# Second norm of an encoder layer: most token rows normed and stored before the last expert pair ends, that pair's tokens normed in slot order and scattered

## The chip, the cores and the metric

The kernel runs on one core of one Trainium2 chip. The metric is the device time of one launch in microseconds (us), the median of repeated runs of one program. Engines are named as the profile names them: PE is TensorE (PEld its weight loads), DVE is VectorE, ACT is ScalarE, POOL is GpSimd, and SP is SyncE, which here issues nearly all transfers.

## The reference

One encoder layer on T = 384 tokens (256 prompt tokens and 8 streams of 16), D = 1024, all in f32: a token mixer, a norm (LN1) that gives h, a mixture of 32 experts of which each token takes four, and a second norm (LN2):

```python
h = layer_norm(DEEPNORM_ALPHA * x + m, ln1_g, ln1_b)
f = moe(h.reshape(B * L, D), w_router, b_router, w_gu, b_gu, w_down, b_down).reshape(B, L, D)
y = layer_norm(DEEPNORM_ALPHA * h + f, ln2_g, ln2_b)
...
gu = xb @ w_gu[e] + b_gu[e]              # (1024 -> 2 x 1024)
h = (up + 1.0) * gate * jax.nn.sigmoid(SWIGLU_ALPHA * gate)   # after clamping
return h @ w_down[e] + b_down[e]
```

A token's LN2 needs its mean and variance over all 1024 channels, and so the outputs of all four of its experts. Each expert has 12 MB of weights, of which all must be read: 16 pairs of experts read 16 x 24 MB.

## The kernel before

The tokens stand as NT = 3 tiles of 128 partitions. After the mixer, the kernel goes over 16 pairs of experts (`pair`). An expert has SLOTS = 64 slots for its tokens, so a pair fills the 128 partitions: slots 0 to 63 belong to expert a = 0, slots 64 to 127 to a = 1. `onehot` (tokens by slots) says which token sits in which slot. It is built for the next pair on DVE (`slots_of`), and `gather` on PE multiplies `hid` (which holds h) by it to give `xg`.

In a pair, PE does this in order:

- `gate_up(0)`, in eight chunks c of 128 input channels, and between its chunks 4 and 6 the scatter of the pair before (`combine`: slot outputs `oo_hi` and `oo_lo` times the transposed one-hot `gt`, added into `xy` by DVE in `add_outputs`), and `gates`, which makes `gt` for this pair.
- `gate_up(1)`, with the transposes of expert 0's activations at chunk 4.
- `down(0)`, with expert 1's transposes at chunk 4.
- `gather` for the next pair (not in the last pair).
- `down(1)`.

The matrices' f32 products have 64 stationary columns, one half of the output columns in partitions 0 to 63 of a bank and the other half (`hf`) in partitions 64 to 127. The trace shows each f32 matmul as two instructions.

SP issues the weights in pieces into a ring of 16 rooms of 1 MB (`ring`, `old_rooms`), each into a room as soon as PE has used what lay there (`piece_used`), so up to 16 MB are ordered ahead. All these transfers and the stores of `y` are issued from SP. The last pair's last piece of `w_down` is split in two (`last_low_full` for chunks 4 and 5 of `down(1)`, L541).

`xy` (tokens by channels) starts as ALPHA * h and has every pair's outputs added. In the last pair, before the change, `xy` is split into a high and a low part (ACT at L1298, DVE `low_sums` at L1806), and PE adds these into six banks through an identity (`sums_so_far`, L1056 and L1061). After `down(1)` PE adds the last pair's outputs on top (L1123, L1127), so the banks hold all sums in token order. Then LN2 of all three tiles follows: `half_stats` and `row_stats` on DVE, `row_rstd` on POOL, `centre` (L1883) and `finish` (L1898) on DVE for tiles 1 and 2, ACT (L1349) and POOL (L1407, L1409) for tile 0, tile 2's variance on ACT (`squares`). The six stores of 256 KB are at L614. LN2's gain and offset (`lnp`, 1 MB as broadcast) are loaded by ACT at L1313 late in the last pair.

In this code `last_down` and all names with `late_` are new, and the functions named above for the norm after the loop are gone.

## Time and profile before

| What | us |
| --- | --- |
| Median of 3 runs | 1114.89 (1114.82 to 1115.33) |
| Profiled execution, own device time | 1111.98 |
| Profiled execution, span (first to last instruction) | 1109.9 |
| PE busy in the span | 1070.8 |
| Mean granted TensorE clock | 0.996 |
| DMA mean rate over the span | 393 GB/s |
| Last instruction of the last `down(1)` ends | 1094.05 |
| First store of `y` issued | 1102.51 |

All positions in the trace are us from the start of the span. A timeline row gives the start, the time that the run of instructions is busy, the engine, the line, the operation and its tiles and shapes, how many, and in brackets the engine's idle time before it and what ended it. Consecutive matmuls overlap, so the duration of one is longer than its share.

### The profile page before, as it was taken

How to read it: one execution, taken by the hardware profiler on the slowest of the kernel's cores; microseconds unless marked ns; L12 is line 12 of the kernel's file. 1: busy time of each engine (PE TensorE's matmuls, PEld its weight loads, DVE VectorE, ACT ScalarE, POOL GpSimd, SP SyncE). 2: the span in 40 equal slices, each digit the busy share in tenths (PEclk: the TensorE clock that was granted, in tenths of full speed). 3: DMA queues.
4: the chain of work that ended last, by engine and by line, in shares of the span. 5: the costliest groups of instructions: out<-in, count | busy, mean ns of one | idle time of the engine just before them, and what ended most of it. 6: DMA issues, size and time to landing. Idle time of an engine off the chain costs nothing.

```text
span 1109.9 us, 13640 instructions
## 1 busy us (share of the span) xinstructions
PE 1070.8 (96%) x5552; PEld 543.4 (49%) x5552; DVE 327.8 (30%) x601; ACT 207.4 (19%) x361; POOL 90.2 (8%) x50
## 2 busy tenths in 40 slices
PE   9999999999999999999999999999898989898995
PEld 6889988353434343444443434343434343342532
DVE  3487765512121212121213121212131312112134
ACT  3243334120202020202020101020111111110122
POOL 4675500000000000000000000000000000000002
PEclk9999999999999999999999999999999999999998
DMA  9972778999999999999999999999999999999994
GB/s 351 324 244 76 247 306 347 393 424 411 427 429 424 430 427 427 427 426 429 428 428 428 427 429 427 427 429 429 427 429 427 427 429 429 425 428 430 425 428 193
DMA packets 56611, 436.27 MB, mean 393 GB/s; under 512 B 8128, under 2 KB 18112, under 8 KB 29088
## 3 DMA queue, kind: packets, MB, share of 16 engines
q1 hardware_dynamic: 50048, 428.68, 93.2%
q10 hardware_dynamic: 6528, 7.09, 1.9%
q8 instruction: 26, 0.43, 0.2%
q14 instruction: 9, 0.07, 0.0%
HBM read 431.78 MB, written 3.97 MB: 393 GB/s over the span
## 4 chain that ended last, share of the span: by engine, by line
PE 67%; DMA 25%; DVE 1%; issue 0%; POOL 0%; ACT 0%; POOLq 0%; SPq 0%; DVEq 0%
PE bank L1014 25%; DMA ring<-w_down 25%; PE bank L1046 18%; PE bank L946 8%; PE bank L639 5%; PE bank L1075 1%; PE bank L995 1%; PE bank L866 1%; PE bank L1077 1%; PE bank L1023 1%; PE bank L856 1%; PE bank L802 1%; PE bank L782 1%; PE bank L788 1%; PE bank L805 1%; PE bank L806 1%
## 5 line engine op out<-in xcount | busy, mean ns | idle before, releaser
L1014 PE MATMUL bank<-ring,xg 128*64 128x512 f32 x1536 | 345.3, 595 | 7.3 <-DMA ring<-w_gu 7.1
L1014 PEld LDWEIGHTS bank<-ring,xg 128*64 128x64 f32 x1536 | 105.0, 136 | 209.1 <-issue 187.9
L1046 PE MATMUL bank<-ring,act_t 128*64 128x512 f32 x672 | 151.0, 595 | 8.3 <-DMA ring<-w_down 8.3
L1014 PE MATMUL bank<-old_rooms,xg 128*64 128x512 f32 x496 | 112.4, 595 | 4.9 <-DMA old_rooms<-w_gu 4.9
L1786 DVE SCALAR_TENSOR_TENSOR oo_lo<-oo_raw,gate_s,oo_hi 128x512 fp32r<-128x512 f32 x32 | 24.0, 751 | 309.7 <-ACT oo_hi L1290 309.7
L1822 DVE TENSOR_SCALAR gate_c<-bank 128x512 f32<-128x512 f32 x32 | 22.1, 691 | 251.3 <-PE bank L1014 251.3
L946 PEld LDWEIGHTS bank<-onehot,hid 128*128 128x128 f32 x720 | 85.9, 196 | 12.2 <-issue 12.2
L1046 PEld LDWEIGHTS bank<-ring,act_t 128*64 128x64 f32 x672 | 46.1, 137 | 92.8 <-issue 78.0
L946 PE MATMUL bank<-onehot,hid 128*128 128x128 f32 x720 | 88.8, 283 | 0.0
L1800 DVE TENSOR_TENSOR xy<-xy,bank 128x512 f32<-128x512 f32 x84 | 52.7, 682 | 107.6 <-PE bank L1077 107.6
L1382 POOL TENSOR_TENSOR rstd<-veps,minus_half 128x1 f32<-128x1 f32 x6 | 3.3, 544 | 960.3 <-DVE veps L1582 960.0
L1365 POOL TENSOR_TENSOR w_parts<-ring,w_parts 128x1024 fp32r<-128x1024 f32 x27 | 74.5, 2762 | 52.9 <-ACT w_parts L1161 52.9
L1014 PEld LDWEIGHTS bank<-old_rooms,xg 128*64 128x64 f32 x496 | 34.1, 136 | 68.2 <-issue 57.4
L1317 ACT COPY oo_raw<-bank 64x512 f32<-64x512 f32 x63 | 36.5, 580 | 159.9 <-PE bank L1046 159.1
L1046 PE MATMUL bank<-old_rooms,act_t 128*64 128x512 f32 x256 | 58.4, 595 | 4.1 <-DMA old_rooms<-w_down 4.1
L1301 ACT ACTIVATE sig<-gate_c 128x512 f32<-128x512 f32 x32 | 20.2, 630 | 179.1 <-DVE gate_c L1822 179.1
L1303 ACT COPY act_t<-bank 128x512 f32<-128x512 f32 x32 | 18.7, 585 | 165.7 <-PE bank L995 165.7
L1279 ACT CAST gt<-bank 128x384 fp32r<-128x384 f32 x16 | 7.7, 479 | 201.2 <-PE bank L958 201.2
L639 PE MATMUL bank<-w_parts,x_hi 128*128 128x512 f32 x180 | 45.1, 397 | 0.0
L1161 ACT CAST w_parts<-ring 128x1024 fp32r<-128x1024 f32 x27 | 28.4, 1053 | 65.8 <-PE bank L639 60.3
L1075 PE MATMUL bank<-oo_hi,gt 128*128 128x512 f32 x90 | 38.5, 428 | 0.0
L639 PEld LDWEIGHTS bank<-w_parts,x_hi 128*128 128x128 f32 x180 | 33.7, 187 | 8.8 <-issue 0.8
(258 smaller groups left out, 940.1 us busy)
## 6 DMA issues: line engine op xcount, KB each, us to landing
ring<-w_gu SPq DMA_DIRECT2D x90, 2048.0 KB, 30.5
ring<-w_down SPq DMA_DIRECT2D x41, 2048.0 KB, 33.0
old_rooms<-w_gu SPq DMA_DIRECT2D x30, 2048.0 KB, 30.3
old_rooms<-w_down SPq DMA_DIRECT2D x18, 1024.0 KB, 26.4
old_rooms<-w_down SPq DMA_DIRECT2D x7, 2048.0 KB, 32.1
ring<-w_in SPq DMA_DIRECT2D x13, 1024.0 KB, 14.5
ring<-w_gu SPq DMA_DIRECT2D x12, 1024.0 KB, 6.2
over_q<-w_down SPq DMA_DIRECT2D x3, 2048.0 KB, 15.9
```

The source lines that it names most:

```text
L639: mm = pe.matmul(out, lhs, rhs, start=(n == 0 and c == 0), stop=(n == 2 and c == KC - 1))
L946: mm = pe.matmul(bank[6 + c // 4][:, (c % 4) * 128:(c % 4 + 1) * 128], hid[:, t, :].rearrange("p (q m k) -> p q k m", m=128, k=GU_RUN) [:, ...
L1014: mm = pe.matmul(bank[2 * a + n][64 * hf:64 * hf + 64, :], xg[:, c, 64 * a:64 * a + 64], w[:, col:col + 512], start=False, stop=(c == KC - 1))
L1046: mm = pe.matmul(bank[b][64 * hf:64 * hf + 64, :], act_t[:, a, c % 4, 64 * (c // 4):64 * (c // 4) + 64], w[:, c % run, hf * 512:(hf + 1) * ...
L1075: pe.matmul(bank[comb_banks[i]][:, :], gt[:, t * 128:(t + 1) * 128], oo_hi[:, hf, :], start=True, stop=False)
L1161: act.copy(w_parts[:, n % PARTS, 0, :], w).then_inc(w_hi_ready, 1)
L1301: act.activation(sig[:, :], gate_c[:, :], ACT.Sigmoid, scale=SIG).then_inc(sig_ready, 1)
L1317: act.copy(oo_raw[64 * a:64 * a + 64, hf, :], bank[down_banks[a]][64 * hf:64 * hf + 64, :]).then_inc(out_ready, 1)
L1365: pool.tensor_tensor(w_parts[:, n % PARTS, 1, :], w, w_parts[:, n % PARTS, 0, :].bitcast(F32), ALU.subtract).then_inc(w_lo_ready, 1)
L1786: dve.scalar_tensor_tensor(oo_lo[:, hf, :], oo_raw[:, hf, :], gate_s[:, 0:1], oo_hi[:, hf, :].bitcast(F32), ALU.mult, ALU.subtract).then_i ...
L1800: dve.tensor_tensor(xy[:, t, o], xy[:, t, o], bank[comb_banks[i]][:, :], ALU.add)\
L1822: dve.tensor_scalar(gate_c[:, :], bank[2 * a][:, :], LIMIT, None, ALU.min).then_inc(gate_ready, 1)
```

## The change

The last pair is no longer scattered by PE into token order. Instead:

- **Norm tables.** ACT loads only one row each of gain and offset (8 KB) at the start of the pair before the last. PE spreads them over 128 partitions by products with a row of ones (`last_norm_rows`, at chunks 2 and 6 of that pair's `gate_up(1)`), and ACT copies them to `lnp`.
- **Rows without the last pair.** In the last pair DVE takes the statistics of `xy` (`row_norm`), norms all three tiles (`norm_early`) and SP stores them whole (three stores of 512 KB), also the rows of tokens that the last pair still changes.
- **Slots.** `gates` is left out in the last pair. PE makes small tables instead (`late_slots`): each slot's token number and gates, and which slots of the two experts hold the same token. `late_rows` gathers each slot's sum so far from `xy`. `last_down` does the product of expert 1 in column halves q of 256 (in bank 5 and bank 7), so that the half q = 0 is complete before q = 1.
- **Norm in slot order.** A slot's row of 1024 lies as two halves of 512 in partitions s and 64 + s. Expert 0's slots are normed first (`late_norm(0)`), and what expert 0 adds to a token that is in expert 1 too goes over by `late_cross`. Half rows' statistics are brought together by small products with the identity (`late_stats`). Expert 1's slots follow.
- **Scatter.** POOL writes the two sets of 128 half rows (256 KB each) to `y` with two indirect transfers, once the three plain stores have landed. Slots that must not be written have an index out of bounds.

The split of `xy` into high and low parts, `sums_so_far`, the products at L1123 and L1127, and everything after the loop are gone.

```diff
+        pe_gain, pe_offset, pe_slots, pe_rows, pe_cross, pe_half, pe_moments = (1, 2), (3, 4), 5, (6, 7), 8, 10, (9, 11)
+        act_gain, act_offset, act_values, act_rows, act_split, act_scaled = 1, 2, 3, (4, 5), 6, 7
+        dve_table, dve_index, dve_stats, dve_rows = 1, 2, (3, 5), (4, 6)
+        last_banks = (5, 7)
...
-            for t, n in ((1, 0), (1, 1), (0, 0), (2, 0), (2, 1), (0, 1)):
-                if t == 0:
-                    sp.wait_ge(y_pool, n + 1)
-                else:
-                    sp.wait_ge(y_done, 2 * (t - 1) + n + 1)
-                o = slice(n * 512, (n + 1) * 512)
-                sp.dma_start(y_out[t * 128:(t + 1) * 128, o], xy[:, t, o]).then_inc(rows_stored, 16)
-            sp.wait_ge(rows_stored, 16 * (2 * NT + 1))
+            for t in range(NT):
+                sp.wait_ge(y_done, 2 * t + 2)
+                sp.dma_start(y_out[t * 128:(t + 1) * 128, :], xy[:, t, :]).then_inc(rows_stored, 16)
+            sp.wait_ge(rows_stored, 16 * (NT + 1))
+            sp.wait_ge(late_stored, 32)
...
+            def last_down(turn):
+                for q in range(2):
+                    for hf in range(2):
+                        pe.matmul(bank[last_banks[q]][64 * hf:64 * hf + 64, 0:256], sel_down[:, 1, :],
+                                  biasp[:, 2 * FF + hf * 512 + q * 256:2 * FF + hf * 512 + q * 256 + 256],
+                                  start=True, stop=False)
+                for c in range(KC):
+                    if c == 4:
+                        late_cross()
...
+                        order = [(k, q) for q in range(2) for k in (c, c + 1)]
+                    elif c < KC - 2:
+                        order = [(c, q) for q in range(2)]
+                    else:
+                        order = []
+                    for k, q in order:
+                        for hf in range(2):
+                            col = hf * 512 + q * 256
+                            mm = pe.matmul(bank[last_banks[q]][64 * hf:64 * hf + 64, 0:256],
+                                           act_t[:, 1, k % 4, 64 * (k // 4):64 * (k // 4) + 64],
+                                           w[:, k % DN_RUN, col:col + 256], start=False, stop=(k == KC - 1))
+                        if (k, q) == (KC - 1, 0):
+                            mm.then_inc(late_pe, 1)
+                    if c % 2 == 1:
+                        mm.then_inc(piece_used, 1)
...
+            def late_slots():
+                pe.wait_ge(late_dve, dve_table)
+                for e in range(2):
+                    for hf in range(2):
+                        for t in range(NT):
+                            pe.matmul(bank[6 + e][64 * hf:64 * hf + 64, 0:4], onehot[:, t, 64 * e:64 * e + 64],
+                                      late_tab[:, t, :], start=(t == 0), stop=(t == NT - 1))
-                    pe.matmul(bank[last_banks[2 * t + hf]][:, :], ident_r, sums_hi[:, t, hf * 512:(hf + 1) * 512],
-                              start=True, stop=False)
-                pe.wait_ge(sums_lo_ready, t + 1)
+                    for t in range(NT):
+                        mm = pe.matmul(bank[5][64 * hf:64 * hf + 64, 0:SLOTS], onehot[:, t, 0:64],
+                                       onehot[:, t, 64:128], start=(t == 0), stop=(t == NT - 1))
+                mm.then_inc(late_pe, 1)
+            row_ones = cst[0:1, C_IOTA + 1:C_IOTA + 2].to_broadcast([1, 128])
+            def late_rows(e):
+                if e == 0:
+                    pe.wait_ge(late_act, act_values)
+                for t in range(NT):
+                    for hf in range(2):
+                        mm = pe.matmul(bank[6 + e][64 * hf:64 * hf + 64, :], onehot[:, t, 64 * e:64 * e + 64],
+                                       xy[:, t, hf * 512:(hf + 1) * 512], start=(t == 0), stop=(t == NT - 1))
+                mm.then_inc(late_pe, 1)
+            def last_norm_rows(n, p):
+                if n == 0:
+                    pe.wait_ge(ln2_in, 16)
+                    pe.wait_ge(gate_ready, 2 * p + 1)
+                    pe.wait_ge(up_ready, 2 * p + 1)
+                else:
+                    pe.wait_ge(late_act, act_gain)
-                    o = slice((2 * t + hf) * 512, (2 * t + hf + 1) * 512)
-                    pe.matmul(bank[last_banks[2 * t + hf]][:, :], ident_r,
-                              x_lo[:, :, :].rearrange("p k t -> p (k t)")[:, o], start=False, stop=False)
+                    pe.matmul(bank[hf][:, :], row_ones, lnp[0:1, n, hf * 512:(hf + 1) * 512], start=True, stop=True)\
+                        .then_inc(late_pe, 1)
+            def late_stats(e):
+                pe.wait_ge(late_dve, dve_stats[e])
+                w = 6 * (1 + e)
+                for half in range(2):
+                    for hf in range(2):
+                        mm = pe.matmul(bank[1 + e][64 * hf:64 * hf + 64, w * half:w * half + w],
+                                       ident[:, 64 * half:64 * half + 64], late_stat[:, e, 0:w], start=True, stop=True)
+                mm.then_inc(late_pe, 1)
+            def late_cross():
+                pe.wait_ge(late_act, act_scaled)
+                for hf in range(2):
+                    r = slice(64 * hf, 64 * hf + 64)
+                    mm = pe.matmul(bank[0][r, :], late_same[r, :], late_out[r, :], start=True, stop=True)
+                mm.then_inc(late_pe, 1)
+                late_stats(0)
...
+                        {4: lambda: upper_and_combine(p), 6: lambda: combine_and_slots(p)} if last else
...
-                        | ({2: lambda: sums_so_far(0), 6: lambda: sums_so_far(1)} if last else {})
+                        | ({1: lambda: late_rows(0), 2: lambda: late_rows(1)} if last else {})
+                        | ({2: lambda: last_norm_rows(0, p), 6: lambda: last_norm_rows(1, p)} if tables else {})
...
+                    late_stats(1)
...
+            def norm_tables(n):
+                for hf in range(2):
+                    act.wait_ge(late_pe, (pe_gain, pe_offset)[n][hf])
+                    ins = act.copy(lnp[:, n, hf * 512:(hf + 1) * 512], bank[hf][:, :])
+                ins.then_inc(late_act, 1)
+            def pair(p, first=False, tables=False):
+                if tables:
+                    act.dma_start(lnp[0:1, :, :], ln2.rearrange("(a n) d -> a n d", a=1)).then_inc(ln2_in, 16)
...
+            def last_pair_of(p):
+                act.wait_ge(late_pe, pe_slots)
+                for e in range(2):
+                    act.copy(late_val[:, e, :], bank[6 + e][:, 0:4])
+                act.copy(late_same, bank[5][:, 0:SLOTS]).then_inc(late_act, 1)
+                activations(p, 0)
+                act.wait_ge(xg_ready, 2 * p)
+                for e in range(2):
+                    act.wait_ge(late_pe, pe_rows[e])
+                    act.copy(late_x[e], bank[6 + e][:, :]).then_inc(late_act, 1)
+                copy_act_t(p, 0)
+                act.wait_ge(late_act, act_offset)
+                for hf in range(2):
+                    r = slice(64 * hf, 64 * hf + 64)
+                    ins = act.copy(late_gb[r, :, :], lnp[r, :, hf * 512:(hf + 1) * 512])
+                ins.then_inc(late_act, 1)
+                activations(p, 1)
+                copy_act_t(p, 1)
+                act.wait_ge(late_act, act_values)
+                act.wait_ge(piece_used, PAIR_PIECES * p + MIX_PIECES + 2 * GU_PIECES + DN_PIECES)
+                act.activation(late_out, bank[down_banks[0]][:, :], ACT.Copy, scale=late_val[:, 0, 2:3])\
+                    .then_inc(late_act, 1)
...
+            for e in range(2):
+                pool.wait_ge(ln_var, 2 * NT + e + 1)
+                pool.tensor_tensor(late_rstd[:, e:e + 1], late_ve[:, e:e + 1], minus_half[:, 0:1], ALU.pow)\
+                    .then_inc(ln_rstd, 1)
+            rows = y_out.rearrange("t (h n) -> (t h) n", h=2)
+            pool.wait_ge(late_dve, dve_index)
+            pool.wait_ge(rows_stored, 16 * (NT + 1))
+            for e, done in enumerate((late_sum, up_c[:, :])):
+                pool.wait_ge(late_dve, dve_rows[e])
+                pool.indirect_dma_start(rows, bass.IndirectOffsetOnAxis(ap=late_idx[:, e:e + 1], axis=0), done, None,
+                                        bounds_check=2 * T - 1, oob_is_err=False).then_inc(late_stored, 16)
...
+            def row_norm(t):
+                for n in range(2):
+                    ins = dve.bn_stats(stat[:, t, n, :], xy[:, t, n * 512:(n + 1) * 512])
+                link(ins)
+                row_stats(t, NT + t + 1)
+            def norm_early(t):
+                dve.wait_ge(late_act, act_gain)
+                for n in range(2):
+                    o = slice(n * 512, (n + 1) * 512)
+                    dve.scalar_tensor_tensor(xy[:, t, o], xy[:, t, o], mv[:, t, 0:1], lnp[:, 0, o],
+                                             ALU.subtract, ALU.mult).then_inc(y_centred, 1)
+                dve.wait_ge(ln_rstd, NT + t + 1)
+                dve.wait_ge(late_act, act_offset)
+                for n in range(2):
+                    o = slice(n * 512, (n + 1) * 512)
+                    dve.wait_ge(y_centred, 2 * t + n + 1)
+                    dve.scalar_tensor_tensor(xy[:, t, o], xy[:, t, o], rstd[:, t:t + 1], lnp[:, 1, o],
+                                             ALU.mult, ALU.add).then_inc(y_done, 1)
+            def row_index():
+                dve.wait_ge(late_act, act_values)
+                for e in range(2):
+                    ins = dve.tensor_tensor(late_idx[:, e:e + 1], late_val[:, e, e:e + 1], late_half, ALU.add)
+                ins.then_inc(late_dve, 1)
+            def late_norm(e, done):
+                s = bank[(6, 3)[e]][:, :]
+                dve.wait_ge(late_pe, pe_moments[e])
+                link(dve.bn_aggr(late_mv[:, e, :], bank[1 + e][:, 0:12 * (1 + e)]))
+                dve.tensor_scalar_add(late_ve[:, e:e + 1], late_mv[:, e, 1:2], EPS).then_inc(ln_var, 1)
+                link(dve.scalar_tensor_tensor(s, s, late_mv[:, e, 0:1], late_gb[:, 0, :], ALU.subtract, ALU.mult))
+                dve.wait_ge(ln_rstd, 2 * NT + e + 1)
+                dve.scalar_tensor_tensor(done, s, late_rstd[:, e:e + 1], late_gb[:, 1, :], ALU.mult, ALU.add)\
+                    .then_inc(late_dve, 1)
+            def late_outputs(p):
+                dve.wait_ge(late_act, act_scaled)
+                link(dve.tensor_tensor(bank[6][:, :], late_out, late_x[0], ALU.add))
+                dve.bn_stats(late_stat[:, 0, 0:6], bank[6][:, :]).then_inc(late_dve, 1)
+                dve.wait_ge(late_pe, pe_cross)
+                link(dve.tensor_tensor(late_x[1], late_x[1], bank[0][:, :], ALU.add))
+                late_norm(0, late_sum)
+                for q in range(2):
+                    o = slice(256 * q, 256 * q + 256)
+                    if q == 0:
+                        dve.wait_ge(late_pe, pe_half)
+                    else:
+                        dve.wait_ge(piece_used, PAIR_PIECES * p + MIX_PIECES + PAIR_PIECES)
+                    link(dve.scalar_tensor_tensor(bank[3][:, o], bank[last_banks[q]][:, 0:256], late_val[:, 1, 3:4],
+                                                  late_x[1][:, o], ALU.mult, ALU.add))
+                    ins = dve.bn_stats(late_stat[:, 1, 6 * q:6 * q + 6], bank[3][:, o])
+                ins.then_inc(late_dve, 1)
+                late_norm(1, up_c[:, :])
```

How this moves instructions: first PE in the last pair, from the end of `combine` to the start of `down(0)`. Before (`gates` is L955 and L958, `sums_so_far` L1056 and L1061):

```order
L955 MATMUL bank<-gate,onehot 128x2 x3
L958 MATMUL bank<-cst,onehot 128x128 x3
L1014 MATMUL bank<-old_rooms,xg 64x512 x8
L1099 REGISTER_ALU
L866 MATMUL bank<-biasp,sel 64x512 x4
L1014 MATMUL bank<-old_rooms,xg 64x512 x8
L1056 MATMUL bank<-over_r 128x512 x2
L1061 MATMUL bank<-x_lo,over_r 128x512 x2
L1014 MATMUL bank<-ring,xg 64x512 x8
L995 MATMUL bank<-cst,act_h 128x128 x4
L1014 MATMUL bank<-ring,xg 64x512 x8
```

And after (L1107 and L1111 are `late_slots`, L1123 `late_rows`):

```order
L1107 MATMUL bank<-rank_all,onehot 64x4 x12
L1111 MATMUL bank<-onehot 64x64 x6
L1026 MATMUL bank<-old_rooms,xg 64x512 x8
L1200 REGISTER_ALU
L878 MATMUL bank<-biasp,sel 64x512 x4
L1026 MATMUL bank<-old_rooms,xg 64x512 x4
L1123 MATMUL bank<-xy,onehot 64x512 x6
L1026 MATMUL bank<-old_rooms,xg 64x512 x4
L1123 MATMUL bank<-xy,onehot 64x512 x6
L1026 MATMUL bank<-ring,xg 64x512 x8
```

Six matmuls of `gates` became 18 small ones, and eight of `sums_so_far` (two turns of four) became twelve f32 ones with 64 stationary columns.

The end of PE's program, from expert 1's down product on. Before:

```order
L1023 MATMUL bank<-biasp,sel_down 64x512 x2
L1046 MATMUL bank<-ring,act_t 64x512 x8
L1038 ISA
L1046 MATMUL bank<-old_rooms,act_t 64x512 x8
L1123 MATMUL bank<-oo_hi,gt 128x512 x3
L1127 MATMUL bank<-oo_lo,gt 128x512 x3
L1123 MATMUL bank<-oo_hi,gt 128x512 x3
L1127 MATMUL bank<-oo_lo,gt 128x512 x3
```

And after (L1093 is `last_down`, L1154 `late_cross`, L1145 `late_stats`):

```order
L1068 MATMUL bank<-biasp,sel_down 64x256 x4
L1093 MATMUL bank<-ring,act_t 64x256 x16
L1154 MATMUL bank<-hid,rank_all 64x512 x2
L1145 MATMUL bank<-rank_all,cst 64x6 x4
L1078 ISA
L1093 MATMUL bank<-old_rooms,act_t 64x256 x16
L1145 MATMUL bank<-rank_all,cst 64x12 x4
```

The twelve products that scattered the last pair are gone from behind the down product. Two products of `late_cross` and four small ones stand in its middle, and only four small ones behind it.

POOL's last rows. Before:

```order
L1382 TENSOR_TENSOR rstd<-veps,minus_half 128x1 x5
L1407 TENSOR_TENSOR xy<-xy,lnp 128x512
L1409 TENSOR_TENSOR xy<-xy,lnp 128x512
L1382 TENSOR_TENSOR rstd<-veps,minus_half 128x1
L1407 TENSOR_TENSOR xy<-xy,lnp 128x512
L1409 TENSOR_TENSOR xy<-xy,lnp 128x512
```

And after (`late_rstd` lies in `rank_all`, L1517 are the two scatters):

```order
L1502 TENSOR_TENSOR gg<-wr,ln_t 128x8x32 x2
L1487 TENSOR_TENSOR rstd<-veps,minus_half 128x1 x6
L1510 TENSOR_TENSOR rank_all<-rank_all,minus_half 128x1 x2
L1517 DMA y<-hid,late_idx 768x512
L1517 DMA y<-up_c,late_idx 768x512
```

POOL's four passes over tile 0 are gone, and both scatters stand behind both powers, the second scatter behind the first.

## Rows read from the trace of the kernel before

**Rows 1.** The page, part 1: busy time, share, instructions.
```profile
PE 1070.8 (96%) x5552; PEld 543.4 (49%) x5552; DVE 327.8 (30%) x601; ACT 207.4 (19%) x361; POOL 90.2 (8%) x50
```

**Rows 2.** Timeline of PE, pair ahead of the last: start, us, engine, line.
```profile
1000.07 7.31 PE L1014 MATMUL bank<-ring,xg 128*64 128x512 f32 x32
...
1008.61 3.65 PE L1014 MATMUL bank<-ring,xg 128*64 128x512 f32 x16 [0.56 <-DMA ring<-w_gu]
1013.51 3.65 PE L1014 MATMUL bank<-old_rooms,xg 128*64 128x512 f32 x16 [1.25 <-DMA old_rooms<-w_gu]
...
1018.42 3.65 PE L1046 MATMUL bank<-old_rooms,act_t 128*64 128x512 f32 x16 [1.03 <-DMA old_rooms<-w_down]
...
1023.32 3.65 PE L1046 MATMUL bank<-ring,act_t 128*64 128x512 f32 x16 [0.57 <-DMA ring<-w_down]
```

**Rows 3.** Windows of the stream's end: busy us, clock, DMA share, GB/s.
```profile
1084.00:1086.00 2.00, 2.00 (x10) 0.99 (x12) 0.00 (x0) 0.00 (x0) 0.00 (x0) 1.00 1.01 422
...
1091.00:1092.00 1.00, 1.00 (x8) 0.31 (x6) 0.00 (x0) 0.00 (x0) 0.00 (x0) 1.00 0.02 8
```

**Rows 4.** Timeline of PE, last pair.
```profile
1053.94 0.72 PE L955 MATMUL bank<-gate,onehot 128*128 128x2 f32 x6
...
1054.98 3.65 PE L1014 MATMUL bank<-old_rooms,xg 128*64 128x512 f32 x16
...
1062.43 0.73 PE L1056 MATMUL bank<-over_r 128*128 128x512 f32 x2
...
1063.56 3.65 PE L1014 MATMUL bank<-ring,xg 128*64 128x512 f32 x16
...
1077.17 3.65 PE L1046 MATMUL bank<-ring,act_t 128*64 128x512 f32 x16 [0.77 <-DMA ring<-w_down]
...
1082.05 1.94 PE L1046 MATMUL bank<-ring,act_t 128*64 128x512 f32 x8 [0.55 <-DMA ring<-w_down]
```

**Rows 5.** The chain that ended last, last pair.
```profile
1047.52 34.49 DMA ring<-w_down
...
1087.19 6.89 PE bank L1046 x32
```

**Rows 6.** Lines by form, PE: count, busy us, mean ns.
```profile
L946 PE MATMUL bank<-onehot,hid 128*128 128x128 f32 x720 | 88.8, 283 | 0.0
...
L725 PE MATMUL bank<-st,hid 128*32 128x128 f32 x64 | 2.6, 279 | 0.0
```

**Rows 7.** Lines by form, DVE.
```profile
L1603 DVE BATCH_NORM_STATS2 stat<-hid 128x6 f32<-128x512 f32 x6 | 4.2, 695 | 0.2
...
L1516 DVE BATCH_NORM_STATS2 gst<-bank 128x6 f32<-128x128 f32 x12 | 2.7, 283 | 2.7 <-PE bank L725 2.7
...
L1571 DVE SCALAR_TENSOR_TENSOR qkt<-bank,chn,zu 128x256 f32<-128x256 f32 x4 | 1.9, 476 | 7.0 <-PE bank L639 7.0
```

**Rows 8.** Timeline of the tail, all engines.
```profile
1098.99 0.21 DVE L1581 BATCH_NORM_AGGREGATE mv<-stat 128x2 f32<-128x12 f32 x1
...
1099.23 0.15 DVE L1582 TENSOR_SCALAR veps<-mv 128x1 f32<-128x1 f32 x1
...
1099.47 0.54 POOL L1382 TENSOR_TENSOR rstd<-veps,minus_half 128x1 f32<-128x1 f32 x1 [916.66 <-DVE veps L1582]
...
1100.43 1.41 DVE L1883 SCALAR_TENSOR_TENSOR bank<-bank,mv,lnp 128x512 f32<-128x512 f32 x2
...
1101.35 1.26 POOL L1407 TENSOR_TENSOR xy<-xy,lnp 128x512 f32<-128x512 f32 x1 [0.22 <-ACT xy L1349]
1101.74 1.40 DVE L1898 SCALAR_TENSOR_TENSOR xy<-bank,rstd,lnp 128x512 f32<-128x512 f32 x2
```

**Rows 9.** The page, part 5: the longest elementwise on POOL.
```profile
L1365 POOL TENSOR_TENSOR w_parts<-ring,w_parts 128x1024 fp32r<-128x1024 f32 x27 | 74.5, 2762 | 52.9 <-ACT w_parts L1161 52.9
```

**Rows 10.** The stores of y at L614: issue ns, landing us.
```profile
L614 SPq DMA_DIRECT2D y<-xy x6: 332/333/357, 1102.5 to 1107.4; - x6
...
DMA to landing us min/median/max: 2.0/2.1/2.1
```

227 lines of the change are left out of this document (89 added, 138 removed).

## The prediction

> **What bounds the kernel now.** I read the page first: PE is busy for 1070.8 of 1109.9 us [rows 1], so on the average the kernel looks PE-bound. The chain that ended last says more: in the last pair, a transfer of `w_down` holds it for 34.49 us, and then a down product on PE for 6.89 us, from 1087.19 to 1094.08 [rows 5]. The PE timeline of the pair ahead of the last shows the same from PE's side: PE stands still four times for weights, 0.56, 1.25, 1.03 and 0.57 us, 3.41 us in all [rows 2]. The loop there is bound by the weight stream, with 3.4 us of room on PE. The windows show the stream at 422 GB/s and a DMA share of 1.01 up to 1086, then draining, and at a share of 0.02 from 1091 on [rows 3]. So the last weights are there at about 1091.9, while PE still has work until 1094.08. In the last pair PE waits only 0.77 and 0.55 us [rows 4], 1.32 in all; work added to PE there beyond this moves the end. Behind 1094.08 come 15.8 us in which no weights move: a serial tail of scatter, norm of three tiles and stores, in which DVE is the busiest engine [rows 8]. The change acts on this tail (shorter) and on PE's work in the last two pairs (longer). I cost both.
>
> **The pair ahead.** `last_norm_rows` adds four f32 matmuls with 128 stationary columns and 512 moving ones. One f32 instruction that moves 128 columns takes 88.8 / 720 = 0.123 us [rows 6], and a matmul is two of them; the 32-instruction down product with 64 stationary columns gives 6.89 / 32 = 0.215 us per instruction [rows 5], and two such stand side by side in the two halves of the columns, so a 128-column one of 512 takes 0.43. Eight instructions: 3.4 us, half at chunk 2 of `gate_up(1)` and half at chunk 6. The waits that follow are 0.56 (at chunk 4), 1.25 (chunk 6) and 1.03 (start of `down(0)`) [rows 2]. By my walk through them PE comes 1.7 - 0.56 = 1.2 us late to chunk 4, 1.2 + 1.7 - 1.25 = 1.7 late behind chunk 6 and 1.7 - 1.03 = 0.6 late into `down(0)`; the wait of 0.57 at 1023.32 takes that. I count 0, with at most 0.5 us left over. What hides it is the weight stream; without that cover it would cost 3.4. Later use of rooms by 1.7 us holds up orders that lie in a queue tens of us deep (34.49 us in the chain), so the stream itself does not thin. ACT's four copies there and its load of 8 KB are off the path.
>
> **PE in the last pair.** Taken away: `gates`, from 1053.94 to the next product at 1054.98, 1.04 us; `sums_so_far` from 1062.43 to 1063.56, 1.13 us [rows 4], three times, 3.38. The 1.32 us of waits vanish too, since PE comes later than the weights from there on. Together 5.74. Added:
>
> - `late_slots`: 18 small f32 matmuls, 36 instructions. The trace has none with 64 stationary columns and so few moving ones. With 128 columns an instruction takes 0.123, with 32 columns 2.6 / 64 = 0.041 [rows 6]. In proportion, 64 columns take 0.068: 36 x 0.068 = 2.45 us (bounds 1.5 and 4.4).
> - `late_rows`: 12 matmuls, 24 instructions of just the shape of the down product, 24 x 0.215 = 5.16 us.
> - `late_cross`: two matmuls of 512 columns, four instructions x 0.215 = 0.86 us (0.43 if the two halves run fully beside each other), and `late_stats(0)`, eight small instructions, 8 x 0.068 = 0.54.
> - `last_down` in halves: twice the instructions at half the columns; I take no change, since a load for a 64-column product of 0.068 fits under 0.107.
>
> Sum added 9.01. PE ends the down product at 1094.08 - 5.74 + 9.01 = 1097.35. I call this E; its bounds are 1095.7 and 1099.7 (all small instructions at 0.041 or at 0.123). PE then reaches chunks 6 and 7 at E - 1.7 = 1095.6, far behind the last weights at 1091.9, so the stream no longer matters there.
>
> DVE has `row_norm` in place of `low_sums` (six statistics of 0.695 [rows 7] and three pairs of small ones, 5.5 us against 3.5), and `norm_early` with 12 passes of about 0.7, some 8.8 us, from about 1069 to 1078. Both lie under `gate_up(1)`, whose result DVE must fetch at about 1080. They cost nothing; if `norm_early` ended later than 1080, each us of it would hold `act_h` and then the transposes at chunk 4 of `down(0)`, which have some 0.8 us to spare. The stores of `y` stand behind the last weights on SP's queue and land at about 1092 to 1096, before the scatter needs them.
>
> **The tail behind E.** DVE is in the half q = 0 until about E + 0.1 (0.476 for the pass over 256 columns [rows 7], and a statistic over 256 columns, between 0.283 for 128 and 0.695 for 512, 0.42). Half q = 1: 0.48 + 0.42 and two hand-overs of 0.05: E + 1.07. `late_stats(1)` on PE: hand-over 0.1, 0.54, and some 0.14 (my estimate) until the last result is out: E + 1.85. Aggregate 0.21, `veps` 0.15 with gaps: E + 2.3. Then DVE centres (0.70) and scales (0.70, with the hand-over 0.8) [rows 8]: rows ready at E + 3.85. POOL's power of 0.54 starts 0.1 after `veps` and is done at E + 2.95. Before, the same chain ran three times over with passes of 512 on more tiles.
>
> **The scatter.** No indirect transfer is in the trace. Its price has two parts: how long POOL is held by one, and how long it takes to land. For the first the nearest rows are SP's issue of a 256 KB store, 0.333 us [rows 10], and POOL's own passes: 0.54 for one word per partition, 1.26 for 128 x 512 [rows 8], 2.76 for 128 x 1024 with a conversion [rows 9]. It is work of POOL over 128 rows, so I take 1.26, with 0.33 and 2.76 as the bounds. POOL meets the first scatter only behind the second power, at E + 2.95, and holds it to E + 4.2; the second follows to E + 5.5. Landing: the stores of the same 256 KB took 2.1 us from issue [rows 10], 1.8 of them behind the issue: E + 7.3. From the last landing (1107.4 + 2.1 = 1109.5) to the span's end are 0.4: E + 7.7 = 1105.05. Against 1109.9 this is 4.85 us less. The page of the Trainium skill "DMA: Bandwidth & Descriptors", section "Anatomy of one DMA — SWDGE (gpsimd) path", gives 2.0 us plus bytes over 436 GB/s for such a transfer and calls descriptor generation small; an estimate by that page is 2.6 us behind E + 3.85, an end at E + 6.85 and 5.7 us less, where my rows give 4.85. No row here shows which is right.
>
> The profiled execution took 1111.98 with a span of 1109.9; I forecast 1107.1 for its like. It lies 2.9 us under the median of the runs, 1114.89, and I carry this difference over: 1114.89 - 4.85 = 1110.0 us.
>
> **Rivals.**
>
> - *The scatter is dear, and the gain is lost in it.* With X us of POOL for each scatter the end is E + 2.95 + 2X + 1.8 + 0.4 = 1102.5 + 2X. Above X = 2.6 us the gain is under 0.2% (2.2 us, about what a measurement of this kernel can tell from no change). At 3.5 it gives 1109.5, 1114.5 by the median. For it: POOL is slow in this trace (2.76 us for one pass), and the first use of an operation may be slow. Against: 128 rows are few, and only one pass of POOL's here is that long. 0.14.
> - *Slower: the same mechanism over its other threshold.* From X = 4.8 us (1102.5 + 2X above 1112.1) the kernel is slower by over 0.2%. At X = 6 it ends at 1114.5, 1119.5 by the median. It would need some 40 ns for each of 128 rows on POOL. 0.06.
> - *The stores get among the last weights.* 1.5 MB at 422 GB/s [rows 3] are 3.7 us: the last weights land at 1095.6 rather than 1091.9, just when PE reaches chunk 6. It costs at most 1 or 2 us, an end at 1106 to 1107, 1111 to 1112 by the median. For it: they are ordered some 15 us ahead of the weights' landing. Against: they stand behind them in one queue. 0.08.
> - *PE gets by more cheaply, or the scatter does.* E at 1095.7 and X at 0.33 (then the rows' readiness rules, E + 3.85 + 0.33 + 2.2): 1102.1, 1107.1 by the median. 0.12.
> - *The forecast*, 1110.0, own range 1108.3 to 1111.8: 0.60.
>
> **How the numbers follow.** The range 1107.2 to 1113.6 holds the forecast, the third and nearly all of the fourth, and the nearer part of the first, where X is just over 2.6: a bit over 0.8. Faster by over 0.2% (below 1112.7): 0.60 + 0.08 + 0.12 = 0.80. Within 0.2%: 0.14. Slower: 0.06.
>
> **What would show it.** In the changed kernel's trace: waits of PE for weights in the pair ahead near 0 and `late_slots` starting at 1053.9 as `gates` does now (right) or later (wrong); no wait for weights in the last pair; `late_slots` 2.5 us, `late_rows` 2.6 twice; the down product's end at 1097.4; DVE's last pass ending at E + 3.85; POOL 1.3 us in each scatter; the span's end at E + 7.7. The forecast fails if POOL needs over 2.6 us for a scatter, if the first scatter is held by a late landing of the stores, or if DVE's `norm_early` reaches past 1081.

## The result and the profile after

The median went from 1115.11 us (1114.82 to 1115.40, four runs) to 1108.42 us (1107.62 to 1108.76, four runs), a ratio of 0.9948 with a 95% interval of 0.9934 to 0.9961: 5.8 us faster. The forecast was 1110.0 with an own range of 1108.3 to 1111.8, 4.85 us faster. The profiled execution took 1108.76 with a span of 1106.6; the forecast for it was 1107.1 and 1105.05. The page of the changed kernel, part 1, beside [rows 1]:

```profile
PE 1077.5 (97%) x5641; PEld 552.3 (50%) x5641; DVE 334.0 (30%) x624; ACT 202.6 (18%) x350; POOL 88.5 (8%) x50
```

The spans of the two profiled executions differ by only 3.3 us (1109.9 and 1106.6). Part of the gain was lost early in the changed kernel's execution, where the change touches nothing (up to 300 us both traces show the same instructions). Windows there (busy us by engine, clock, DMA share, GB/s), first the changed kernel:

```profile
186.00:190.00 4.00, 4.00 (x22) 3.93 (x22) 1.91 (x11) 2.33 (x5) 0.00 (x0) 0.57 1.02 422
...
232.00:236.00 4.00, 4.00 (x18) 1.39 (x16) 0.00 (x0) 0.59 (x1) 0.00 (x0) 0.73 1.01 432
```

And the kernel before:

```profile
186.00:190.00 4.00, 4.00 (x37) 3.93 (x37) 1.90 (x12) 2.27 (x5) 0.00 (x0) 1.00 1.01 428
...
232.00:236.00 4.00, 4.00 (x24) 1.32 (x22) 0.00 (x0) 1.16 (x2) 0.00 (x0) 1.00 1.05 444
```

At a granted clock of 0.57 only 22 matmul instructions ran where 37 did. Such dips come and go between executions of one kernel: the kernel before, profiled again, had 0.58 in 228 to 232 us where it first had 1.00, and the changed kernel had 1.00 in 186 to 190 us the second time. So I count from a mark behind them: PE's wait for a piece of `w_gu` near 950 us, in the loop that both kernels share and that the stream paces. Before:

```profile
949.81 3.65 PE L1014 MATMUL bank<-ring,xg 128*64 128x512 f32 x16 [0.57 <-DMA ring<-w_gu]
```

After:

```profile
951.74 2.79 PE L1026 MATMUL bank<-ring,xg 128*64 128x512 f32 x12 [0.56 <-DMA ring<-w_gu]
```

From this mark to the end of the span it is 160.09 us before and 154.86 after, 5.23 less; the loop was reached 1.93 later in the changed kernel's execution, which leaves the 3.3. All comparisons below go by this distance. From the mark on, landings that PE waits for stand on a beat of 4.90 us (in [rows 2, 4] the waits at 1008.61 and 1082.05 end 15 beats of 4.896 apart), so one can also say how far a landing is off the beat.

**The pair ahead.** Timeline of PE after, from `gate_up(1)` on (L1136 is `last_norm_rows`), beside [rows 2]:

```profile
1005.54 1.98 PE L1136 MATMUL bank<-lnp,cst 1*128 1x512 f32 x4
1007.45 3.65 PE L1026 MATMUL bank<-ring,xg 128*64 128x512 f32 x16
...
1015.29 1.98 PE L1136 MATMUL bank<-lnp,cst 1*128 1x512 f32 x4
1017.20 3.65 PE L1026 MATMUL bank<-old_rooms,xg 128*64 128x512 f32 x16
...
1020.91 3.60 PE L1058 MATMUL bank<-old_rooms,act_t 128*64 128x512 f32 x16
...
1025.24 1.94 PE L1058 MATMUL bank<-ring,act_t 128*64 128x512 f32 x8
```

Eight instructions hold PE for 2 x 1.91 = 3.82 us (from 1005.54 to 1007.45 and from 1015.29 to 1017.20), and all four waits of 3.41 us are gone. The last pair starts 90.04 us behind the mark, before 90.06: nothing is left over. That 3.82 fit under 3.41 is no contradiction. The bracket gives the idle time behind the modelled end of the instruction before, while the starts leave room of 0.6, 1.3, 1.2 and 0.6 us, about 3.8 in all (my estimate from the starts in the trace of before).

**The last pair**, beside [rows 4, 5]; L1107 and L1111 are `late_slots`, L1123 `late_rows`, L1154 `late_cross`, L1145 `late_stats`, L1093 `last_down`:

```profile
1041.78 0.60 PE L878 MATMUL bank<-biasp,sel 96*64 96x512 bf16 x4
...
1046.35 3.65 PE L1026 MATMUL bank<-ring,xg 128*64 128x512 f32 x16 [0.54 <-DMA ring<-w_gu]
...
1056.69 0.89 PE L1107 MATMUL bank<-rank_all,onehot 128*64 128x4 f32 x22
...
1057.96 3.60 PE L1026 MATMUL bank<-old_rooms,xg 128*64 128x512 f32 x15
...
1063.37 2.91 PE L1123 MATMUL bank<-xy,onehot 128*64 128x512 f32 x12
1065.95 2.05 PE L1026 MATMUL bank<-old_rooms,xg 128*64 128x512 f32 x8
...
1090.39 3.67 PE L1093 MATMUL bank<-ring,act_t 128*64 128x256 f32 x32 [0.55 <-DMA ring<-w_down]
1094.00 1.08 PE L1154 MATMUL bank<-hid,rank_all 64*64 64x512 f32 x4
1095.00 0.40 PE L1145 MATMUL bank<-rank_all,cst 128*64 128x6 f32 x8
1095.26 3.65 PE L1093 MATMUL bank<-old_rooms,act_t 128*64 128x256 f32 x32
```

The two waits are the surprise; because of the first, `late_slots` starts 104.95 us behind the mark, where `gates` started at 104.13. E, the end of the down product, is 1095.26 + 3.65 = 1098.91, 147.17 behind the mark; before it was 1090.45 + 3.60 = 1094.05, 144.24 behind. So E moved by 2.93, against 3.27 forecast.

**The tail**, all engines, beside [rows 8]:

```profile
1098.97 0.48 DVE L1973 SCALAR_TENSOR_TENSOR bank<-bank,rank_all,hid 128x256 f32<-128x256 f32 x1
1099.49 0.43 DVE L1975 BATCH_NORM_STATS2 rank_all<-bank 128x6 f32<-128x256 f32 x1
...
1099.97 0.41 PE L1145 MATMUL bank<-rank_all,cst 128*64 128x12 f32 x8 [1.06 <-DVE rank_all L1975]
1100.43 0.27 DVE L1952 BATCH_NORM_AGGREGATE rank_all<-bank 128x2 f32<-128x24 f32 x1 [0.51 <-PE bank L1145]
1100.73 0.15 DVE L1953 TENSOR_SCALAR rank_all<-rank_all 128x1 f32<-128x1 f32 x1
...
1100.97 0.54 POOL L1510 TENSOR_TENSOR rank_all<-rank_all,minus_half 128x1 f32<-128x1 f32 x1 [4.10 <-DVE rank_all L1953]
1101.61 0.75 DVE L1956 SCALAR_TENSOR_TENSOR up_c<-bank,rank_all,hid 128x512 f32<-128x512 f32 x1
1101.91 1.19 POOL L1517 DMA_INDIRECT y<-hid,late_idx  x1 [0.40 <-issue]
1103.41 0.97 POOL L1517 DMA_INDIRECT y<-up_c,late_idx  x1 [0.30 <-issue]
```

Source lines of the changed kernel, the scatters (landing us), beside [rows 10]:

```profile
DMA to landing us min/median/max: 2.7/2.7/2.7
```

The tail is 7.69 us behind E instead of 15.85. POOL meets the first scatter when its second power is done, and POOL rules the end: the second scatter starts at 1103.41, 1.05 behind the ready rows (1102.36), and 3.2 us later the span ends.

### The profile page after: what moved, and what is told of

It reads as the page before. It is cut to its first block, busy times and chain, and to the rows that moved or that the text cites. A ratio compares the mean times of both kernels' runs of the same rounds, so it can differ in the third digit from the quotient of the medians.

```text
span 1106.6 us, 13819 instructions
## 1 busy us (share of the span) xinstructions
PE 1077.5 (97%) x5641; PEld 552.3 (50%) x5641; DVE 334.0 (30%) x624; ACT 202.6 (18%) x350; POOL 88.5 (8%) x50
## 4 chain that ended last, share of the span: by engine, by line
PE 67%; DMA 25%; issue 1%; DVE 0%; POOLq 0%; POOL 0%; SPq 0%
PE bank L1026 26%; DMA ring<-w_down 22%; PE bank L1058 16%; PE bank L958 7%; PE bank L651 5%; DMA ring<-w_gu 3%; PE bank L1169 1%; PE bank L1171 1%; PE bank L1007 1%; PE bank L878 1%; PE bank L868 1%; PE bank L1035 1%; PE bank L814 1%; PE bank L794 1%; PE bank L800 1%
## 5 line engine op out<-in xcount | busy, mean ns | idle before, releaser
L1058 PE MATMUL bank<-ring,act_t 128*64 128x512 f32 x656 | 147.1, 594 | 6.5 <-DMA ring<-w_down 6.4
L958 PEld LDWEIGHTS bank<-onehot,hid 128*128 128x128 f32 x720 | 85.9, 196 | 12.2 <-issue 12.2
L958 PE MATMUL bank<-onehot,hid 128*128 128x128 f32 x720 | 88.8, 283 | 0.0
L1058 PE MATMUL bank<-old_rooms,act_t 128*64 128x512 f32 x240 | 55.9, 605 | 3.1 <-DMA old_rooms<-w_down 3.1
```

The lines of the kernel that those rows point to most:

```text
L958: mm = pe.matmul(bank[6 + c // 4][:, (c % 4) * 128:(c % 4 + 1) * 128], hid[:, t, :].rearrange("p (q m k) -> p q k m", m=128, k=GU_RUN) [:, ...
L1058: mm = pe.matmul(bank[b][64 * hf:64 * hf + 64, :], act_t[:, a, c % 4, 64 * (c // 4):64 * (c // 4) + 64], w[:, c % run, hf * 512:(hf + 1) * ...
```

## The experiments

All distances in this table are from the mark near 950 us; "off" is how far the landings that PE waits for in the last two pairs stand behind the beat.

| Kernel | time, us (runs) | last pair starts | E | tail | end | off |
| --- | --- | --- | --- | --- | --- | --- |
| before | 1115.11 (4) | 90.06 | 144.24 | 15.85 | 160.09 | 0.0 |
| b_again | 1115.09 (12) | 90.03 | 144.63 | 15.87 | 160.50 | 0.4 |
| after | 1108.42 (4) | 90.04 | 147.17 | 7.69 | 154.86 | 1.5 |
| a_again | 1106.64 (6) | 90.08 | 147.27 | 7.64 | 154.91 | 1.6 |
| a_fourth | 1106.34 (6) | 90.04 | 147.17 | 7.67 | 154.84 | 1.5 |
| c_pool_order | 1107.15 (6) | 90.03 | 147.11 | 7.84 | 154.95 | 1.5 |
| d_no_plain | 1108.69 (8) | 90.03 | 147.16 | 7.66 | 154.82 | 1.5 |
| x1_no_rows | 1107.33 (1) | 90.04 | 145.66 | 7.62 | 153.28 | 0.0 |
| x2_no_load | 1107.29 (1) | 90.03 | 145.63 | 7.64 | 153.27 | no wait |
| x2c_again | 1105.99 (1) | 90.04 | 147.20 | 7.67 | 154.87 | 1.5 |
| x3_rows_twice | 1112.21 (1) | 95.04 | 150.65 | 7.64 | 158.29 | no wait |
| x4_row_early | 1105.24 (1) | 90.15 | 146.62 | 7.71 | 154.33 | 1.0 |
| x4b_timed | 1107.94 (6) | 90.02 | 145.85 | 7.71 | 153.56 | no wait |
| f2_one_product | 1105.65 (1) | 90.94 | 146.55 | 8.64 | 155.19 | 0.9 |

b_again is the kernel before; all others below it are the changed kernel or edits of it. No gain is read from the time of a single run.

**The two kernels again** (b_again and a_again, no edit).

> The kernel before, unchanged, beside itself. Theory: the profiled execution of before (1111.98 us, no stretch of low granted clock ahead of the tail) was one of the quicker ones, and others lose up to some 3 us of TensorE clock ahead of the weight-bound part, as the changed kernel's did at 186 to 190 us (0.57) and 228 to 236 us (0.84, 0.73). Then the runs here spread between about 1112 and 1115.5 with clocks from 0.996 down. Rival: its runs are all near 1115 with a trace like the first, and the 3 us lie outside the span. Ratio 1.000 in both.

> The changed kernel again. Theory: the tail behind the down product is some 7.7 us in place of 15.8 and the last pair 2.9 us longer, so 5 us less in like executions; ratio about 0.9950, with span differences between executions coming from granted clock below 1 ahead of 640 us. Rival: the 6.7 us of the medians are real and come from a second place; then a trace without low clock would end near 1103.

Beside the kernel before (1113.32, 19 runs), b_again gave a ratio of 1.0012 (0.9999 to 1.0025) and a_again 0.9937 (0.9918 to 0.9956); a_fourth, beside 1115.02 (11 runs), gave 0.9923 (0.9907 to 0.9939). So 7.0 and 8.6 us by these, and 5.8 by the first; the kernel before against itself differs by 1.3. By the mark it is 160.3 (mean of two) to 154.87 (mean of three): 5.4 us. But all three executions of the changed kernel have landings 1.5 us off the beat, and the two of before 0.0 and 0.4. Where the landings of a changed kernel kept within 0.2 us of the beat (x1, x2, x4b), its distance is 153.27 to 153.56, which is 6.5 to 6.8 below 160.09. So 5.4 us is what these executions had, and up to 6.8 what like landings give.

On b_again's theory: its runs spread from 1110.92 to 1116.0 us, and its trace has the dip at 228 us, so dips come without the change too. But its mark lies at 949.70, no later than in the first trace of before (949.81), so this dip does not explain the 3 us between the first profiled execution (1111.98) and the median. They stay open.

On a_again's rival, a second place of gain: traces whose clock was 1.00 in 186 to 190 and in 228 to 236 us have a span of 1109.9 before, and with the change 1104.0 (c_pool_order), 1103.9 (x2c_again), 1103.2 (x4_row_early) and 1102.0 (x4b_timed), which is 5.9 to 7.9 less. Of this 5.1 to 6.5 lie behind the mark. The other 0.8 to 1.4 lie ahead of it, and with a single such trace of before it stays open whether that is more than chance.

**The order of POOL's last steps** (c_pool_order): the first scatter ahead of the second power.

```diff
-            for e in range(2):
+            for e, done in enumerate((late_sum, up_c[:, :])):
                 pool.wait_ge(ln_var, 2 * NT + e + 1)
...
-            pool.wait_ge(late_dve, dve_index)
-            pool.wait_ge(rows_stored, 16 * (NT + 1))
-            for e, done in enumerate((late_sum, up_c[:, :])):
+                if e == 0:
+                    pool.wait_ge(late_dve, dve_index)
+                    pool.wait_ge(rows_stored, 16 * (NT + 1))
```

> On POOL the first scatter goes ahead of the second power. Theory: the first scatter starts when the plain stores have landed (about 1098.5 in the position of the changed kernel's trace) and is over before the second power is wanted, so the second scatter starts at the end of its rows, about 1.0 us earlier than now: 0.7 to 1.1 us faster than the changed kernel. Rival: the second scatter's start waits for the first one's landing or for a slow hand-over on POOL; then no gain.

The tail became 7.84, not shorter. All engines at its end:

```profile
1097.24 1.19 POOL L1517 DMA_INDIRECT y<-hid,late_idx  x1 [3.13 <-DVE rank_all L1975]
...
1098.46 0.58 POOL L1511 TENSOR_TENSOR rank_all<-rank_all,minus_half 128x1 f32<-128x1 f32 x1
1099.14 0.75 DVE L1956 SCALAR_TENSOR_TENSOR up_c<-bank,rank_all,hid 128x512 f32<-128x512 f32 x1 [0.34 <-POOL rank_all L1511]
1100.73 1.04 POOL L1517 DMA_INDIRECT y<-up_c,late_idx  x1 [1.69 <-DVE up_c L1956]
```

The first scatter did go earlier, but it made the power and so DVE's last pass 0.34 late. What held it was the plain stores: their last landing in this trace is at 1096.27, and it started 0.97 later, with its rows ready since 1094.97. And the second scatter started 0.84 us behind the ready rows (1099.14 + 0.75 = 1099.89) with POOL idle. So both scatters of this kernel began 0.84 to 0.97 us after the last thing that they waited for. In the changed kernel the same time is there but covered: the small MOVE that the trace shows ahead of each scatter (L1517) starts at 1101.0 and 1102.4, 0.9 and 1.0 us ahead of it, while POOL still does the power or the first scatter, and only 0.30 to 0.40 of it shows as idle. The gain that I expected from a free POOL was this hand-over.

**The plain stores left out** (d_no_plain).

```diff
-                sp.dma_start(y_out[t * 128:(t + 1) * 128, :], xy[:, t, :]).then_inc(rows_stored, 16)
-            sp.wait_ge(rows_stored, 16 * (NT + 1))
+            sp.wait_ge(rows_stored, 16)
...
-            pool.wait_ge(rows_stored, 16 * (NT + 1))
+            pool.wait_ge(rows_stored, 16)
```

> The three plain stores of y are left out (y then lacks all rows but those of the last pair). Theory: their 1.5 MB share the DMA engines with the last weights, so without them the wait of 0.55 us for w_down ahead of the last down product goes, and the down product ends 0.5 us earlier: 0.3 to 0.7 us faster than the changed kernel. Rival one: they stand behind the weights and cost nothing: no difference. Rival two: the scatters' 2.7 us to landing also shrink: 1 us or more.

PE's wait stays (it is even longer), E is the same, and so is the scatters' landing of 2.7 us. So the stores are not among the last weights and cost nothing. Timeline of PE, and the window in which the stream of weights alone runs out:

```profile
1090.53 3.67 PE L1092 MATMUL bank<-ring,act_t 128*64 128x256 f32 x32 [1.03 <-DMA ring<-w_down]
```

```profile
1092.50:1095.00 2.50, 2.50 (x20) 1.06 (x16) 0.00 (x0) 0.00 (x0) 0.00 (x0) 1.00 0.06 26
```

A DMA share of 0.06 is that of one of 16 engines: one works about 2.5 us longer than the rest. The kernel before ends in a share of 0.04 for 1 us, from 1090.5.

**The norm rows and their load** (x1_no_rows, x2_no_load, x3_rows_twice, x4_row_early). In this order: the four products move 2 columns instead of 512; the load is left out, with PE's wait for it; each product stands twice; the rows are loaded at the kernel's start into two unused partitions, and the products take them from there.

```diff
-                    pe.matmul(bank[hf][:, :], row_ones, lnp[0:1, n, hf * 512:(hf + 1) * 512], start=True, stop=True)
+                    pe.matmul(bank[hf][:, 0:2], row_ones, lnp[0:1, n, hf * 512:hf * 512 + 2], start=True, stop=True)
```
```diff
-                    act.dma_start(lnp[0:1, :, :], ln2.rearrange("(a n) d -> a n d", a=1)).then_inc(ln2_in, 16)
+                    pass
```
```diff
+                    pe.matmul(bank[hf][:, :], row_ones, lnp[0:1, n, hf * 512:(hf + 1) * 512], start=True, stop=True)
                     pe.matmul(bank[hf][:, :], row_ones, lnp[0:1, n, hf * 512:(hf + 1) * 512], start=True, stop=True)
```
```diff
+            act.dma_start(ln2_rows[3 * E:3 * E + 2, 0:D], ln2).then_inc(ln2_in, 16)
...
-                    pe.matmul(bank[hf][:, :], row_ones, lnp[0:1, n, hf * 512:(hf + 1) * 512], start=True, stop=True)\
+                    pe.matmul(bank[hf][:, :], cst[3 * E:3 * E + 2, C_SEL + n:C_SEL + n + 1].to_broadcast([2, 128]),
+                              ln2_rows[3 * E:3 * E + 2, hf * 512:(hf + 1) * 512], start=True, stop=True)\
...
-                    act.dma_start(lnp[0:1, :, :], ln2.rearrange("(a n) d -> a n d", a=1)).then_inc(ln2_in, 16)
+                    pass
```

> The products that spread gain and offset are cut to 2 of 512 columns each (the tables in the output norm are then not the right ones); the load of 8 KB by ACT stays. In all traces of the changed kernel the landing that the last down product waits for is 1.5 us later than 28 beats of 4.898 us behind the landing of w_gu near 950 us; before the change it kept the beat to 0.0 to 0.4 us. Theory A (PE's norm rows make rooms free later and the stream loses it): the 1.5 us are gone here. Theory B (the 8 KB load onto one partition holds one DMA engine up): they stay.

> ACT's load of gain and offset is left out (the products spread what lies in that row of lnp, so the tables are not the right ones). Theory A (late rooms): the landing ahead of the last down product stays 1.5 us behind the beat. Theory B (the load): it is on the beat, and the down product's end comes 0.5 to 1.0 us earlier, until PE's own work binds.

> Each of the four products that spread gain and offset is done twice: 3.6 us more of PE in the pair ahead. The first 3.4 us are hidden under waits for weights, so these are not: the last pair starts later by up to 3.4 us against the beat of the stream. Then less room to the weights in the last pair: the down product's end moves 2 to 3.4 us later. Theory A: the landing moves by another 1.5 us or more; theory B: it does not move.

> Gain and offset are loaded at the start of the kernel into two partitions that nothing else uses, and the products take them from there; nothing is loaded in the pair ahead. The output is complete. Theory B: landing on the beat, end 0.5 to 1.0 us earlier than the changed kernel in like stretches. Theory A: no change but noise. Rival: the early load of 8 KB holds up the first weights by a similar 1.5 us and the kernel is no faster.

Without the products (x1) three of the four waits are back in the pair ahead (0.71, 1.02, 0.57) and the last pair starts at the same 90.04: the products are hidden. Doubled (x3), the last pair starts 5.0 late. PE's windows there:

```profile
1020.70:1026.00 5.30, 5.30 (x19) 1.68 (x20) 0.00 (x0) 0.58 (x1) 0.00 (x0) 0.68 0.99 420
```

5.3 x 0.32 = 1.7 of it is a clock of 0.68; the other 3.3 are the second 3.8 us of products, less 0.5. So the cover is used up but for half a microsecond. E moved by 3.5 beside the changed kernel and by 5.0 beside x2, in which PE does not wait in the last pair either; 2 to 3.4 were expected, without the dip of the clock.

In both x1 and x2 the two waits of the last pair vanished, and E fell by 1.5. Theory A is right in x1 alone and theory B in x2 alone, so neither fits both; and with the load moved away (x4) the landing is still 1.0 off. So I ran x2 again.

> As x2_no_load: the 8 KB load of the gain's and offset's rows is left out (so LN2's gain and offset are whatever lay in the row), all else stays. If that load is what puts the weights of the last pair 1.5 us off the stream's beat, the two waits for weights stay away again, and the time from the landing near 950 us to the end is 153.3 us again. If it was chance (the 16 DMA engines drift apart by more in one execution than in another), it is anywhere from 153.3 to 154.9.

The same kernel, without the load, now waited. Timeline of PE in x2c_again:

```profile
1087.72 3.67 PE L1093 MATMUL bank<-ring,act_t 128*64 128x256 f32 x32 [1.03 <-DMA ring<-w_down]
```

In x2_no_load:

```profile
1088.99 3.62 PE L1093 MATMUL bank<-ring,act_t 128*64 128x256 f32 x32
```

So the 1.5 us are a matter of the execution, not of the load. They are worth 153.27 against 154.87 for one kernel.

The trace says more: it records each of the 16 landings of a transfer of weights (its semaphore counts up by 16). Three transfers of 2 MB in a row of the changed kernel, us from the start of the span:

| first landing | 8th | 15th | 16th |
| --- | --- | --- | --- |
| 1021.33 | 1023.13 | 1024.68 | 1025.19 |
| 1026.22 | 1028.02 | 1029.58 | 1031.77 |
| 1031.12 | 1032.92 | 1034.46 | 1036.51 |

Fifteen landings keep the step of 4.90 us. The last one takes 6.58 once, and from then on stands 2 us behind the fifteenth. All 14 traces, the two of before among them, have four such places (and smaller ones, of up to 1.3 us in sum) between the mark and the end of the stream, 54 to 59, 80 to 88, 108 to 109 and 124 to 137 us behind the mark. At each, the 16 landing times together lose 1.4 to 2.0 us against the beat, in some on the last landing alone, as here. In the others the loss goes over the ranks within the 16, as when one landing of the 16 falls back past its neighbours.

What PE waits for is the last landing, and it moves only when the loss falls on it or near it: once by 1.5 to 1.7 in after, a_again, a_fourth, c_pool_order, d_no_plain and x2c_again, by 0.9 in x4_row_early and f2_one_product, by 0.4 and 0.2 in b_again and x4b_timed, and in before, x1, x2 and x3 not at all. In x1, x2 and x3 the last landing had lost its 1.5 us already 430 to 455 us ahead of the mark and still stood 1.6 to 2.1 us behind the fifteenth at the mark (0.2 to 1.1 in the others), so that no other could get behind it. Their mark is late by this, and the distance from it is shorter. Both theories fall with this: the losses come with and without the load, the products and the whole change (x3, with the most products, kept the beat).

> The changed kernel with the rows of gain and offset loaded at the kernel's start, timed in rounds beside the changed kernel. If the time from a landing of the stream near 950 us to the end tells more than chance (154.33 us in the single look against 154.82 to 154.95 in four profiles of the changed kernel's kind), this version stands 0.5 us below the changed kernel, and 5.9 us below the kernel before: a ratio to it of 0.9947. The rival: the 0.5 us is scatter of the stream, this version and the changed kernel give the same, 0.9952, and the intervals (some 0.002 wide) can't tell 0.5 us anyway; then the profile's distance from the landing to the end decides, 154.3 again or 154.9.

> The changed kernel itself once more, as the measure for the other kernels here. From the landing near 950 us to the down product's end 147.1 to 147.3 us as in the four profiles of its kind so far, tail 7.6 to 7.7, ratio to before 0.994 to 0.996. If the two waits for weights in the last pair (0.54 and 0.55) are a matter of chance, they are absent or of another size this time.

x4b_timed: 0.9939 (0.9921 to 0.9956) beside a_fourth's 0.9923 (0.9907 to 0.9939). The early load is no gain; its smaller distances, 154.33 and 153.56, go with its landings, 1.0 off and without a wait.

**The column halves** (f2_one_product): the down product of expert 1 with 512 columns in bank 5; DVE gets both halves at its end.

```diff
-                            mm = pe.matmul(bank[last_banks[q]][64 * hf:64 * hf + 64, 0:256],
-                                           act_t[:, 1, k % 4, 64 * (k // 4):64 * (k // 4) + 64],
-                                           w[:, k % DN_RUN, col:col + 256], start=False, stop=(k == KC - 1))
...
+                        mm = pe.matmul(bank[5][64 * hf:64 * hf + 64, :],
+                                       act_t[:, 1, c % 4, 64 * (c // 4):64 * (c // 4) + 64],
+                                       w[:, c % DN_RUN, hf * 512:hf * 512 + 512], start=False, stop=(c == KC - 1))
```

> Expert 1's down product in the last pair as before the change, 512 columns in one bank, so DVE finds both column halves only at its end. What the halves are worth by the trace of the changed kernel: DVE had the first half behind it 0.1 us after the product's end (0.87 us of work hidden), so the tail here is 7.7 + 0.8 = 8.5 us. The rival: the halves cost PE something (twice the instructions at half the columns), then the product's end comes earlier here, by 0.1 us for each 0.003 us that a 256-column instruction costs over half of a 512-column one, and the total moves by less than 0.8.

The tail is 8.64 instead of 7.67 (0.8 more was expected): the halves bring 0.97 us. E can't be compared directly, since this execution had its late landing in the pair ahead and started the last pair 0.9 late; from that start to E it takes 55.61, as x2 with 55.60. PE and DVE there:

```profile
1091.33 3.63 PE L1086 MATMUL bank<-old_rooms,act_t 128*64 128x512 f32 x16
```

```profile
1095.08 0.49 DVE L1966 SCALAR_TENSOR_TENSOR bank<-bank,rank_all,hid 128x256 f32<-128x256 f32 x1 [1.29 <-PE bank L1086]
1095.61 0.43 DVE L1968 BATCH_NORM_STATS2 rank_all<-bank 128x6 f32<-128x256 f32 x1
```

Sixteen instructions of 512 columns take PE 3.63, thirty-two of 256 took 3.65, so they cost PE nothing. The rival falls.

## Why the prediction was right, and where its terms were off

- **The pair ahead: right.** 3.82 us of products rather than 3.4, all hidden: with them cut to 2 columns (x1) the waits come back and the last pair starts at the same 90.04, and doubled (x3) they are no longer hidden.
- **PE in the last pair: the sum near by luck, from two errors that cancel.** x2_no_load, in which PE never waits there, gives PE's own work: its last pair lasts 145.63 - 90.03 = 55.60 to E, before 144.24 - 90.06 = 54.18. By these two the last pair grew by 1.4, not 3.27. The mis-sized term is above all `late_slots`: 2.45 forecast, 1.15 to 1.3 measured (1056.69 to 1057.84 or 1057.96), some 0.032 us for each of 36 instructions. That is below my lower bound of 1.5, which was 36 at the 0.041 of a 32-column product. `late_rows` took 2.58 twice as forecast, `late_cross` 1.00 (0.86), `late_stats(0)` 0.26 (0.54). That is 1.3 of the 1.9 us; by the starts in the trace of before, the two waits were room of about 1.6 rather than 1.32, and some 0.3 I can't place.
- **"PE comes later than the weights from there on" failed.** With 1.3 us less on PE, PE comes just with the weights. In x2 it starts the first 32 instructions of `last_down` (L1093, 1088.99) 137.16 us behind the mark, and an on-beat landing stands 28 beats or 137.1 us behind it. So a last landing that has moved by 1.5 us makes it wait by that much: E is 1.5 later than in x2. That the waits of 1.32 vanish was true only in executions whose last landing had not moved behind the mark (x1, x2, x3, and x4b, with 0.2).
- **DVE: right.** `norm_early` ran from 1070.61 to 1078.57 and DVE fetched `gate_up(1)` at 1081.75.
- **The stores: right in effect, wrong in time.** They stand behind the weights and cost nothing (d_no_plain), but land 19.2 to 20.4 us after their issue at 1073.4 to 1078.7, the last at 1099.0, not 1096. In c_pool_order, where POOL wants them earlier, this landing holds the first scatter.
- **The tail: right in mechanism and sum, with some luck in the sizes.** E + 7.69 against E + 7.7. Rows are ready at E + 3.45 (forecast 3.85), but don't rule. POOL starts the first scatter at E + 3.00 (2.95) and the second 1.5 later, at E + 4.5 (4.2). It is held for 1.19 and 0.97 us (1.26, a choice between bounds of 0.33 and 2.76), with a gap of 0.30 between them that I had not counted. The landing is 2.7 us from the start, where the terms gave 1.26 + 1.8 = 3.06. So 0.3 too little and 0.36 too much cancel. The rivals of a dear scatter fall. The page of the Trainium skill "DMA: Bandwidth & Descriptors", section "Anatomy of one DMA — SWDGE (gpsimd) path", gives 2.0 us plus bytes over 436 GB/s, 2.6 here, and the trace agrees with 2.7. My estimate by that page, an end at E + 6.85, was too early, because it counts from the ready rows and leaves out what POOL needs to make two scatters in a row.
- **The carried difference.** I added 2.9 us of difference between profile and median to get 1110.0. That difference belonged to one execution, not to the kernel: in the changed kernel the profiled execution (1108.76) is not below the median (1108.42). The forecast gain of 4.85 stands against 5.8 by the medians and 5.2 to 5.4 by the mark.

**What stays open** is why a landing loses its 1.5 us, and on which engine. The stream does not thin: its windows of 8 us between 980 and 1080 show 424 to 434 GB/s in both kernels. The same page, section "Why a DMA increments its semaphore by 16 and not by 1", says that a transfer has landed only when all 16 engines have reported, and the trace agrees in this: a single landing behind makes a transfer late while the mean rate is full. The losses come four times behind the mark with and without the change, so the change does not cause them. In the last pair neither kernel has room for them: E moved by 1.5 with the last landing in the changed kernel, and by 0.4 in b_again, where the last landing moved by 0.4.
